# Plain float32 matmuls in the projections of a hybrid decoder step, in place of products of rounded high and low parts

## The reference, cut to what matters

```python
z = rmsnorm(h, g_mix) @ w_in              # 1024 -> q, k, v (3 x 512), 8 forget logits, 2 x 512 conv, 2 x 1024 gates
q, k, v, fl, ca, cb, ga, gc = split(z)
glu = ca * sigmoid(cb)                    # convolution branch's input
att = attend(q, k, v, logf) @ w_att_proj  # 512 -> 1024
conv = silu(layernorm(dwconv(glu))) @ w_conv_proj
h = h + (sigmoid(ga) * att + sigmoid(gc) * conv) @ w_out
h = h + peer(rmsnorm(h, g_ffn), w_pq, sub_keys, exp_u, exp_v)
h = h + (p_i @ w_ple) * sigmoid(rmsnorm(h, g_ple) @ w_ple_gate)
y = rmsnorm(h, g_final)
```

## Time and profile before

| | |
|---|---|
| median of 3 runs | 5648.16 us (5642.25 to 5650.38) |
| profiled execution, first to last instruction (span) | 5638.5 us |
| the runs' median less the span | 9.7 us |
| mean granted clock of TensorE | 0.815 of full |
| TensorE matmul, busy | 3830.5 us (68%), 14101 instructions |
| VectorE, busy | 2710.5 us (48%) |
| GpSimd, busy | 2646.9 us (47%) |
| ScalarE, busy | 1038.5 us (18%) |

### The profile page before, as it was taken

How to read it: one execution, slowest core, us unless ns; L and a number is a source line. 1 busy time by engine, 2 the same in 40 slices (tenths; PEclk the granted TensorE clock), 3 DMA queues, 4 the chain that set the end, 5 groups by cost and what they waited for, 6 DMA issues and landing times. The chain is left out here.

```text
span 5638.5 us, 57052 instructions
## 1 busy us (share of the span) xinstructions
PE 3830.5 (68%) x14101; PEld 2341.2 (42%) x14101; DVE 2710.5 (48%) x8425; ACT 1038.5 (18%) x2091; POOL 2646.9 (47%) x2596
## 2 busy tenths in 40 slices
PE   6799854554997656676666666766666666766667
PEld 6667831322887523333333333333333333333246
DVE  2233275343112566555655565555555555555433
ACT  2122121111001211122121121121112111121121
POOL 2100222222112056666666666666666666666621
PEclk8855977777998777887888888888888878888879
DMA  2200166663112379999999999999999999999921
GB/s 62 73 23 12 37 227 221 225 237 106 57 46 61 98 253 331 333 327 323 333 331 325 331 328 332 328 327 335 333 324 328 325 329 329 330 328 333 329 90 50
DMA packets 471328, 1331.83 MB, mean 236 GB/s; under 512 B 48641, under 2 KB 141259, under 8 KB 471257
## 3 DMA queue, kind: packets, MB, share of 16 engines
q0 software_dynamic: 326240, 1180.32, 58.3%
q1 hardware_dynamic: 145024, 150.76, 8.7%
HBM read 1307.67 MB, written 23.66 MB: 236 GB/s over the span
## 5 line engine op out<-in xcount | busy, mean ns | idle before, releaser
L1589 PE MATMUL exp_ps_y<-exp_V,exp_diag 128*128 128x512 f32 x4224 | 1978.3, 632 | 1144.0 <-ACT exp_diag L1665 1125.5
L1798 DVE CUSTOM_DVE_ANT_0 exp_U<-exp_U,exp_x 128x1024 f32<-128x1024 f32 x1056 | 1294.4, 1226 | 1179.8 <-DMA exp_U<-in_exp_u,exp_idx_now 1154.9
L1589 PEld LDWEIGHTS exp_ps_y<-exp_V,exp_diag 128*128 128x128 f32 x4224 | 854.2, 204 | 2241.2 <-issue 1925.2
L1545 POOL DMA_INDIRECT exp_V<-in_exp_v,exp_idx_now x1056 | 1055.4, 999 | 735.5 <-PE exp_ps_y L1589 514.0
L1545 POOL DMA_INDIRECT exp_U<-in_exp_u,exp_idx_now x1056 | 1190.4, 1127 | 383.0 <-issue 312.2
L1665 ACT ACTIVATE exp_diag<-all_ident,exp_wt 128x128 f32<-128x128 f32 x1024 | 389.9, 398 | 1186.4 <-PE exp_ps_y L1589 1137.1
L1579 PE MATMUL exp_ps_sc<-ffn_wk,exp_ust 128*128 (+1 forms) x1152 | 276.4, 395 | 36.1 <-ACT exp_scores L1648 36.1
L1659 ACT ACTIVATE exp_act_dots<-exp_dots 128x16 f32<-128x16 f32 x66 | 14.2, 216 | 1384.4 <-DVE exp_dots L1798 1384.4
L1579 PEld LDWEIGHTS exp_ps_sc<-ffn_wk,exp_ust 128*128 128x128 f32 x1152 | 228.0, 199 | 96.6 <-issue 58.0
L1750 DVE SCALAR_TENSOR_TENSOR exp_picked<-exp_iota,exp_tif,exp_cidx 128x70 f32<-128x70 f32 x1152 | 252.8, 290 | 2.6
L999 PE MATMUL satt_ps_o<-satt_pages,satt_kT 128*32 128x512 f32 x512 | 92.8, 889 | 199.7 <-DMA satt_pages<-in_cache_v 197.5
(11 more groups left out here) (309 smaller groups left out, 5107.0 us busy)
## 6 DMA issues: line engine op xcount, KB each, us to landing
satt_pages<-in_cache_k SPq DMA_DIRECT2D x128, 256.0 KB, 4.1
satt_pages<-in_cache_k POOLq DMA_DIRECT2D x128, 256.0 KB, 4.3
satt_pages<-in_cache_v SPq DMA_DIRECT2D x128, 256.0 KB, 6.3
satt_pages<-in_cache_v POOLq DMA_DIRECT2D x128, 256.0 KB, 6.4
exp_U<-in_exp_u,exp_idx_now POOLq DMA_INDIRECT x1056, 6.1
exp_V<-in_exp_v,exp_idx_now POOLq DMA_INDIRECT x1056, 5.6
merge_w<-in_w_in SPq DMA_DIRECT2D x16, 512.0 KB, 4.0
keys_w<-in_w_pq SPq DMA_DIRECT2D x16, 512.0 KB, 4.9
```

The lines of the kernel that those rows point to most:

```text
L1545: pool.indirect_dma_start(buf[:, k % size, :], None, table[0], bass.IndirectOffsetOnAxis(idx_now[:, hh, k:k + 1], 0))\
L1589: last = pe.matmul(yb[f][:, :], diag[:, k % ND, :], V[:, k % NV, f * 512:(f + 1) * 512], start=False, stop=False, skip_group_check=True)
L1798: dve.tensor_tensor_reduce(out=row, in0=row, in1=xb[:, :], scale=1.0, scalar=0.0, op0=ALU.mult, op1=ALU.add, accum_out=dots[:, k:k + 1]).t ...
```

## The change

`SplitProduct` is deleted and the five stages use `Product`. `Product` itself is as before. GpSimd no longer touches weights, ScalarE and VectorE no longer split x, nothing is restored, and TensorE has one float32 matmul where it had three. In `residual_product` TensorE waits for all three chunks of x before its first product. The helpers `placed` and `over`, which put the low parts over x, go as well, and with them the addresses handed to the stages.

```diff
-class SplitProduct(Product):
...
-    def split_weights(self, pool):
-        S = len(self.split)
-
-        def one(i, j, first):
-            at = self.split.index(j)
-            pool.wait_ge(self.loaded[j], 16 * i + 16)
-            if not first or at >= 2:
-                before = WS * i + self.split[at - 2] if at >= 2 else WS * (i - 1) + self.split[at - 2 + S]
-                hold(pool, self.ready, NCH * before + NCH, self.passed_split)
-            raw = self.ring[:, j, 0:self.chunks[j], :]
-            high, low = self.high[:, at % 2, 0:self.chunks[j], :], self.low[:, at % 2, 0:self.chunks[j], :]
-            pool.tensor_copy(high, raw).then_inc(self.w_high, 1)
-            hold(pool, self.w_high, S * i + at + 1, self.passed_split)
-            pool.tensor_tensor(low, raw, high, ALU.subtract).then_inc(self.w_split, 1)
-        for j in self.split:
-            one(0, j, True)
-        with pool.Fori(1, self.turns) as i:
-            for j in self.split:
-                one(i, j, False)
-
-    def x_highs(self, act, loaded=None):
-        for c in range(NCH):
-            if loaded is not None:
-                act.wait_ge(loaded[c], 16)
-            for x, high in zip(self.xs, self.high_tiles):
-                act.activation(high[:, :, cols(c)], x[:, :, cols(c)], ACT.Copy).then_inc(self.x_high, 1)
-
-    def x_lows(self, dve):
-        for c in range(NCH):
-            for n, (x, high, low) in enumerate(zip(self.xs, self.high_tiles, self.low_tiles)):
-                dve.wait_ge(self.x_high, len(self.xs) * c + n + 1)
-                dve.tensor_tensor(low[:, :, cols(c)], x[:, :, cols(c)], high[:, :, cols(c)], ALU.subtract).then_inc(self.x_split, 1)
-
-    def restore(self, eng, lo, hi):
-
-        eng.wait_ge(self.ready, NCH * WS * self.turns)
-        for x, high, low in zip(self.xs, self.high_tiles, self.low_tiles):
-            eng.tensor_tensor(x[:, lo:hi, :], high[:, lo:hi, :], low[:, lo:hi, :], ALU.add)
-
...
-                    if j in self.split:
-                        pe.wait_ge(self.x_split, len(self.xs) * (c + 1))
-                    for k in range(self.chunks[j]):
-                        first, end = k == 0, k == self.chunks[j] - 1
-                        if j not in self.split:
-                            last = pe.matmul(self.bank(j, c), self.ring[:, j, k, :], self.rhs(j, k, c), start=first, stop=end)
-                            continue
-                        slot = self.split.index(j) % 2
-                        w_high, w_low = self.high[:, slot, k, :], self.low[:, slot, k, :]
-                        x_high, x_low = self.rhs(j, k, c)
-                        pe.matmul(self.bank(j, c), w_high, x_high, start=first, stop=False)
-                        pe.matmul(self.bank(j, c), w_high, x_low, start=False, stop=False)
-                        last = pe.matmul(self.bank(j, c), w_low, x_high, start=False, stop=end)
-                    last.then_inc(self.ready, 1)
-
...
-        pr = SplitProduct(nc, s, 3, lambda i, j: w[:, :, ds((WS * i + j) * P, P)], [KD] * WS,
-                          lambda j, k, c: pr.parts_of(0, k, c), [(uT, u_at)], ring=ring, parts_at=v_at)
+        pr = Product(nc, s, 3, lambda i, j: w[:, :, ds((WS * i + j) * P, P)], [KD] * WS,
+                     lambda j, k, c: uT[:, k, cols(c)], ring=ring)
...
-        @block.gpsimd
-        def _(pool):
-            pr.split_weights(pool)
-            pr.restore(pool, 6, KD)
-
         @block.scalar
         def _(act):
-            pr.x_highs(act)
             copy_out(act, (0, 2), lambda o, i: act.activation(o, i, ACT.Copy), passed_a)
 
         @block.vector
         def _(dve):
-            pr.x_lows(dve)
             copy_out(dve, (1, 3), dve.tensor_copy, passed_v)
-            pr.restore(dve, 0, 6)
...
             for c in range(CK):
                 last = dve.tensor_copy(sg[:, 0, c * NS:(c + 1) * NS].rearrange("p (b s) -> p b s", s=SD), gs[:, c, :, PAD:PAD + SD])
             last.then_inc(e["runs_made"], 1)
-            pr.restore(dve, 0, 6)
             dve.wait_ge(e["tok_turned"], 1)
             dve.tensor_copy(tokp[:, :], pb[0][0:PAD, :]).then_inc(e["tok_copied"], 1)
...
         def rhs(j, k, c):
-            return pr.parts_of(0, k, c) if j % 2 == 0 else (attT, yT)[j // 2][:, k, cols(c)]
-        pr = SplitProduct(nc, s, KD, weights, [KD, AC, KD, CK], rhs, [(uT, u_at)], split=(0, 2))
+            return (uT, attT, uT, yT)[j][:, k, cols(c)]
+        pr = Product(nc, s, KD, weights, [KD, AC, KD, CK], rhs)
         sg = s.sb("sg", [P, 2, T])
...
-def residual_product(nc, sh, name, weight, xT, x_at):
+def residual_product(nc, sh, name, weight, xT):
     w = w_view(weight)
     with Scope(nc, name) as s:
-        pr = SplitProduct(nc, s, KD // WS, lambda i, j: w[:, :, ds((WS * i + j) * P, P)], [KD] * WS,
-                          lambda j, k, c: pr.parts_of(0, k, c), [(xT, x_at)])
+        pr = Product(nc, s, KD // WS, lambda i, j: w[:, :, ds((WS * i + j) * P, P)], [KD] * WS,
+                     lambda j, k, c: xT[:, k, cols(c)])
         passed_v, x_loaded = s.sem("passed_v"), [s.sem(f"x_loaded{c}") for c in range(NCH)]
         block = s.block()
-        block.tensor(pr.multiply)
-        block.gpsimd(pr.split_weights)
+
+        @block.tensor
+        def _(pe):
+            for c in range(NCH):
+                pe.wait_ge(x_loaded[c], 16)
+            pr.multiply(pe)
 
         @block.sync
         def _(sp):
...
                     pr.load_one(sp, 0, 0)
             pr.load(sp, 1)
 
-        @block.scalar
-        def _(act):
-            pr.x_highs(act, x_loaded)
-
         @block.vector
         def _(dve):
-            pr.x_lows(dve)
...
```

More of the change, by code:

```diff
@@ L6 @@
 F32 = mybir.dt.float32
-F32R = mybir.dt.float32r
 I32 = mybir.dt.int32
@@ L325, in multiply @@
                     last.then_inc(self.ready, 1)
-class SplitProduct(Product):
[L334 to L351, removed]
-    def split_weights(self, pool):
-        S = len(self.split)
-        def one(i, j, first):
-            at = self.split.index(j)
-            pool.wait_ge(self.loaded[j], 16 * i + 16)
-            if not first or at >= 2:
-                before = WS * i + self.split[at - 2] if at >= 2 else WS * (i - 1) + self.split[at - 2 + S]
-                hold(pool, self.ready, NCH * before + NCH, self.passed_split)
-            raw = self.ring[:, j, 0:self.chunks[j], :]
-            high, low = self.high[:, at % 2, 0:self.chunks[j], :], self.low[:, at % 2, 0:self.chunks[j], :]
-            pool.tensor_copy(high, raw).then_inc(self.w_high, 1)
-            hold(pool, self.w_high, S * i + at + 1, self.passed_split)
-            pool.tensor_tensor(low, raw, high, ALU.subtract).then_inc(self.w_split, 1)
-        for j in self.split:
-            one(0, j, True)
-        with pool.Fori(1, self.turns) as i:
-            for j in self.split:
-                one(i, j, False)
-    def x_highs(self, act, loaded=None):
-        for c in range(NCH):
-            if loaded is not None:
-                act.wait_ge(loaded[c], 16)
-            for x, high in zip(self.xs, self.high_tiles):
-                act.activation(high[:, :, cols(c)], x[:, :, cols(c)], ACT.Copy).then_inc(self.x_high, 1)
-    def x_lows(self, dve):
-        for c in range(NCH):
-            for n, (x, high, low) in enumerate(zip(self.xs, self.high_tiles, self.low_tiles)):
-                dve.wait_ge(self.x_high, len(self.xs) * c + n + 1)
-                dve.tensor_tensor(low[:, :, cols(c)], x[:, :, cols(c)], high[:, :, cols(c)], ALU.subtract).then_inc(self.x_split, 1)
-    def restore(self, eng, lo, hi):
-        eng.wait_ge(self.ready, NCH * WS * self.turns)
-        for x, high, low in zip(self.xs, self.high_tiles, self.low_tiles):
-            eng.tensor_tensor(x[:, lo:hi, :], high[:, lo:hi, :], low[:, lo:hi, :], ALU.add)
[L392 to L401, removed]
-                        if j in self.split:
-                            pe.wait_ge(self.w_split, S * i + self.split.index(j) + 1)
-                    if j in self.split:
-                        pe.wait_ge(self.x_split, len(self.xs) * (c + 1))
-                    for k in range(self.chunks[j]):
-                        first, end = k == 0, k == self.chunks[j] - 1
-                        if j not in self.split:
-                            last = pe.matmul(self.bank(j, c), self.ring[:, j, k, :], self.rhs(j, k, c), start=first, stop=end)
-                            continue
-                        slot = self.split.index(j) % 2
-                        w_high, w_low = self.high[:, slot, k, :], self.low[:, slot, k, :]
-                        x_high, x_low = self.rhs(j, k, c)
-                        pe.matmul(self.bank(j, c), w_high, x_high, start=first, stop=False)
-                        pe.matmul(self.bank(j, c), w_high, x_low, start=False, stop=False)
-                        last = pe.matmul(self.bank(j, c), w_low, x_high, start=False, stop=end)
-                    last.then_inc(self.ready, 1)
```

(8 more changed lines are left out.)

40 lines of the change are left out of this document (13 added, 27 removed).

## The result

| | before | after |
|---|---|---|
| median | 5645.2 us (4 runs, 5622.14 to 5650.38) | 5729.65 us (4 runs, 5719.42 to 5739.43) |
| ratio to before | | 1.0158, 95% interval 1.0136 to 1.0179 |
| span of the profiled execution | 5638.5 us | 5728.2 us |
| mean granted clock | 0.815 | 0.816 |
| TensorE matmul, busy | 3830.5 us, 14101 instructions | 3990.2 us, 12805 |

The changed kernel is slower: by 84 us in the medians (the interval says 77 to 101 us), by 89.7 us in the spans of the two profiled executions. All ratios here are of fast runs; one slow run of the kernel before (10581.06 us), made beside experiments 1 and 2, is in none of them. 1296 x 3 matmuls became 1296 plain ones of two records each, so 1296 instructions fewer. TensorE is busy 160 us longer with fewer instructions, and GpSimd 232 us less, which buys little: it is free in stages that wait for TensorE.

The account below looks back on a forecast made before the run. TensorE was taken to bound the five split-product stages, so its changes enter the span one for one: +148.3 -27.0 -6.7 -10.6 -7.7 -2.7 = +93.6 us, 5742 us as a median, range 5724 to 5764.

Parts of the forecast that it names:

- The stream: Five stages' 1296 products: a plain one costs 0.5913 us against 0.4769 us for three rounded, +148.3 us.
- Rival 1: In the new places a plain product costs a third more than a triple, 0.636 us: 5800 us, chance 0.03.
- rival 4: Plain products among themselves go at one record each, 0.2957 us, so the kernel gets faster: 5359 us, chance 0.03.
- The starts: TensorE no longer waits for the first splits in qkv, glu, merge and gate; out gains a wait: -27.0 us.
- Inside and behind: Gate's TensorE idle time goes, -6.7 us; the restore behind the products goes in qkv, -10.6, and glu, -7.7.
- Cold clock: Each stream starts at half clock, 2.7 us a stage in either form: +0 difference, 1 us either way.
- Small: Qkv's scope end, fewer semaphores to clear, and the next stage's clock kept up by less idling: -2.7 us together.
- The sum: All terms: +93.6 us on a span of 5638.5, 5732; with the 9.7 us margin to the median 5742 us.
- Rivals 2, 3 and 5: Covers stay, 5778 us, chance 0.04; clock drops in long plain streams, 5817, 0.03; TensorE isn't the bound, nothing moves, 0.01.

Follow-up runs that it names:

- experiment 1: Kernel before with one plain float32 matmul in place of three, all splitting and restoring kept: 5795.46 us, ratio 1.0254.
- experiment 2: Kernel before with a fourth rounded matmul (low by low) added: 5842.49 us, ratio 1.0351; in another kernel with the third left out: 5464.96 us, ratio 0.9653.
- experiment 4: Kernel before with the sums that restore uT made chunk by chunk, shared by GpSimd and VectorE: 5633.06 us against 5636.83, ratio 0.999.
- experiment 3: Kernel before with only merge made plain, the other four stages keeping the splits: 5674.8 us, ratio 1.0063.
- experiment 7: Kernel before with a stage behind it of rounded and plain matmul streams at four widths: at 352 columns 160 ns rounded, 592 ns plain.
- experiment 5: Kernel before with the first weight tile of each of the five stages multiplied plain: 5631.44 us, ratio 0.9985.

## Why the prediction was right, point by point

**The stream** (+148.3 us): right but for glu. The plain pitch of 0.5913 us, taken from one pair of consumers in merge, comes again in every stage. The triple's 0.4769 us comes again in out, where a consumer came every 3.82 us; in glu it does not. There the two VectorE consumers shown in experiment 4 for the kernel before, with 16 triples between them, give (701.94-694.20)/16 = 0.484 us. So glu's 192 products took 1.3 us more before than the sum has, and the change costs that much less. What made them slower there no run shows. As to the whole, experiment 1 has +144.6 us in the stages with gate's 5 us of cover in it, 143.3 expected. Rival 1 (equal passes, 5800 us) and rival 4 (one record a product) are answered by experiment 2, by the record counts and by a consumer every 4.73 us in the changed kernel. That the plain pitch would carry from groups of 4 to groups of 8 on one bank holds to 0.001 us.

**The starts** (-27.0): right for qkv, merge and gate, which start 7.8, 7.2 and 5.7 us earlier counted from the stage's first transfer (forecast 7.5, 7.3, 5.6). In out TensorE's added wait ends 17.6 us after the stage begins and not 16.7. In glu TensorE starts 6.3 us after the stage's first transfer, and was to start at 6.5.

**Inside and behind** (-6.7, -10.6, -7.7): gate's idle time is gone, qkv's restore too. Glu's end was worth more than its term, 9.2 us from the last large product of VectorE to the next stage (17.4 us before, 8.2 after) where 7.7 stood. With a stream of 11.5 us more from the stage's start where 13.8 was worked out, this is the 3.8 us that glu is short of its forecast; glu is the only stage off by over 1.5 us. Of the 2.3 us of the second part, 1.3 us are the dearer triples named above, 0.7 us the clock, as follows, and some 0.3 us the earlier start.

**Cold clock** (+0, and 1 us either way for each stream): the prediction took qkv's start, all at 0.50, for that of every stream, 2.7 us each. The first 5.5 us of glu's and out's streams, before and after, in the columns of the earlier trace rows (qkv's stand above, at 0.51):

```profile
606.50:612.00 5.50, 5.47 (x22) 5.47 (x23) 0.00 (x0) 0.00 (x0) 3.34 (x2) 0.62 0.00 0
1706.90:1712.40 5.50, 5.50 (x26) 5.50 (x27) 4.44 (x2) 2.71 (x2) 1.94 (x2) 0.73 1.15 302
```

```profile
614.90:620.40 5.50, 5.50 (x16) 3.51 (x15) 1.61 (x8) 0.00 (x0) 0.00 (x0) 0.75 0.92 229
1766.70:1772.20 5.50, 5.50 (x11) 3.41 (x12) 0.00 (x0) 0.00 (x0) 0.00 (x0) 0.58 0.75 187
```

Only the difference between the kernels counts. Glu lost 5.5 x 0.38 = 2.1 us before and 1.4 after, 0.7 less; out lost 1.5 before and 2.3 after, 0.8 more. Merge stands at 0.74 and 0.72, gate at 0.61 and 0.50 (0.6 us more). The +0 holds as a sum, to 0.8 us, and each stage lies inside the 1 us that was allowed.

**Small** (-2.7): nearly nothing of it came. The scope's end in qkv takes 1.2 us from its last copy to the next stage and not 1.5. The preparation's clock was 0.86 after and 0.89 before, although TensorE had idled 4.8 us and not 15: that a shorter pause would keep the clock up is a mechanism of the sum that failed, and the stages between qkv and glu were 4.7 us longer, not shorter.

**The sum**: +92.0 us in the five stages for +96, +89.7 in the span for +93.6. The measured median is 12 us under the 5742 us forecast, and 8 of these are no mechanism of the change: the margin of 9.7 us between span and median was not the start and end of an execution. The execution profiled after took 5729.78 us with a span of 5728.2, so 1.6 us lie around the span, and at the same 1.6 us the one profiled before was about 5640, 8 us under the median it was held against. That the sum comes within 4 us of the spans' difference is in part luck: the untouched stages moved by +4.7 and -6.8 us, which nearly cancel, and in other executions they moved by more.

**Rivals 2, 3 and 5.** The covers went as counted. The clock held at 1.00 behind the starts. And TensorE is the bound: experiment 2 moves the five stages both ways by the price of the matmul.

**What stays open** is the spread of the stages that nobody touched, which hides effects of 10 us in the whole. Over the eleven profiled executions the second norm, keys and experts took 3632 to 3661 us. In the long stretch of the prompt's attention, before, after and in experiment 3 (columns of the earlier trace rows):

```profile
280.00:591.70 311.70, 288.30 (x1088) 221.28 (x1088) 102.30 (x360) 86.86 (x196) 1.25 (x2) 0.57 0.06 18
```

```profile
292.30:608.60 316.30, 292.67 (x1088) 225.39 (x1088) 102.62 (x360) 86.87 (x196) 1.25 (x2) 0.55 0.07 19
```

```profile
278.50:576.00 297.50, 269.95 (x1088) 206.98 (x1088) 102.19 (x360) 86.80 (x196) 1.25 (x2) 0.61 0.07 21
```

The same 1088 matmuls take 288.30, 292.67 or 269.95 us at a granted clock of 0.57, 0.55 or 0.61, VectorE and ScalarE are busy the same, and the heads' preparation and this attention together last 359, 364 or 345 us. The length goes with the granted clock; which is the cause of which, and what decides between them, no run shows.

## What to carry to other kernels

Price a change of number format by the pitch of consumers of both forms at the width that is used, not by the count of matmuls or passes: here three rounded matmuls of 352 columns (0.477 us) beat one plain float32 matmul (0.591 us), while at 128 columns three of 112 ns would lose to one of 223 ns (experiment 7). The extra work of splitting is hidden by a stream that TensorE bounds, but not at its two ends; before giving the splits up, shorten the ends: a first tile in the plain form and sums made chunk by chunk won 0.6%, where dropping the splits lost 1.6%. A change in a chain of stages that add up is read stage by stage, since untouched stages moved by up to 29 us.

## What the runs showed of the hardware that was not expected

- A rounded matmul of 256, 352 or 512 columns costs its columns at 2.4 GHz and 13 to 14 ns more (106.7+13, 146.7+13, 213.3+14); a record of a plain matmul costs twice its columns and 2.5 ns (213.3, 293.3, 426.7; measured 215.9, 295.8, 429.2). At 128 columns both kinds of record take 112 ns, which is a floor for the rounded one (53.3+13 = 67 without it). What sets the floor was not tested. By this arithmetic the constant, 4 x 13 against 2 x 2.5 ns, is the difference between four rounded matmuls and one plain (0.637 and 0.591 us); why the rounded one has the larger constant no run shows.
- Four VectorE copies of 128x32 elements took 3.87 us while GpSimd summed, and 0.44 us when it did not, in the changed kernel and in experiment 4 alike. The Trainium skill, SBUF — State Buffer, section SBUF: two separate sides, has an exclusive lock between the two engines. The traces agree with it: one copy waited 3.6 us, until GpSimd's sum ended, and the others ran at full speed.
- TensorE's gap of 3.07 us, from 5464.4 to 5467.5, was followed by a stretch at clock 0.55 (experiment 5).
